# Gate and up projections: more steps as seven products of sums, with the split weights also in the residual's place

## The reference

```python
hn2 = rmsnorm(x, norm2_w[l])
gu = hn2 @ w_gate_up[l]                                     # 2048 x 2*5632
x = x + (jax.nn.silu(gu[..., :FFN_HIDDEN]) * gu[..., FFN_HIDDEN:]) @ w_down[l]
...
m = rms_norm(h, ffn_norm_g)
return h + (jax.nn.silu(m @ w_gate) * (m @ w_up)) @ w_down
```

## Time and profile before

| | us |
|---|---|
| median of 3 runs (2575.23 to 2576.02) | 2575.98 |
| the profiled execution's own time | 2576.22 |
| its span, first to last instruction | 2574.4 |

### The profile page before, as it was taken

The page is one execution under the profiler, slowest core; times in us unless marked ns, Lnnn a source line. Parts: engine busy times, 40 slices in busy tenths (PEclk is TensorE's granted clock), DMA queues, the critical chain, the costliest instruction groups (busy, mean ns, idle before and its releaser), DMA issues.

```text
span 2574.4 us, 30659 instructions
## 1 busy us (share of the span) xinstructions
PE 2561.0 (99%) x11740; PEld 2122.9 (82%) x11740; DVE 1603.7 (62%) x1799; ACT 1473.3 (57%) x1811; POOL 824.6 (32%) x368
## 2 busy tenths in 40 slices
PE   9999999999999999999999999999999999999999
PEld 7888888888887888888888888888878888888887
DVE  6798955434347878787533467456477878786222
ACT  7776645445455656566544575565565656566333
POOL 2687753344441000000444455333320000003443
PEclk9999999999999999999999999999999999999999
DMA  8766654466666475656566644554557565655554
GB/s 302 222 209 204 178 192 161 162 223 210 204 203 246 168 250 174 243 184 217 190 215 205 223 168 157 172 196 142 185 194 247 174 243 183 234 194 194 202 203 147
DMA packets 174705, 516.13 MB, mean 200 GB/s; under 512 B 108027, under 2 KB 111068, under 8 KB 117216
## 3 DMA queue, kind: packets, MB, share of 16 engines
q1 hardware_dynamic: 174128, 513.64, 59.9%
q10 hardware_dynamic: 432, 0.52, 0.1%
HBM read 487.38 MB, written 2.10 MB: 190 GB/s over the span
## 4 chain that ended last, share of the span: by engine, by line
PE 94%; DVE 2%; issue 1%; ACT 1%; POOL 1%; DMA 0%; SPq 0%; ACTq 0%; DVEq 0%; POOLq 0%
PE PB L858 18%; PE PB L862 18%; PE PB L859 18%; PE PB L925 8%; PE PB L926 8%; PE PB L929 8%; PE PB L909 2%; PE PB L906 2%; PE PB L904 2%; ACT WH L1460 1%; PE PB L1168 1%; PE PB L1010 0%; DVE WL L2251 0%; PE PB L1040 0%; POOL WL L3321 0%
## 5 line engine op out<-in xcount | busy, mean ns | idle before, releaser
L3321 POOL TENSOR_TENSOR WL<-RAW,WH 128x1024 fp32r<-128x1024 f32 x280 | 703.1, 2512 | 1730.0 <-ACT WH L1460 1729.1
L1460 ACT ACTIVATE WH<-RAW 128x1024 fp32r<-128x1024 f32 x738 | 776.2, 1057 | 797.6 <-PE PB L862 634.3
L2251 DVE TENSOR_TENSOR WL<-RAW,WH 128x1024 fp32r<-128x1024 f32 x456 | 613.6, 1348 | 753.6 <-ACT WH L1460 752.3
L858 PE MATMUL PB<-WH,HNH 128*128 128x512 f32 x1152 | 458.6, 398 | 2.6 <-ACT TM L2036 2.4
L862 PE MATMUL PB<-WL,HNH 128*128 128x512 f32 x1152 | 449.4, 390 | 1.5 <-POOL WL L3321 1.5
L859 PE MATMUL PB<-WH,HNL 128*128 128x512 f32 x1152 | 448.6, 389 | 0.0
L858 PE MATMUL PB<-WH,HDH 128*128 128x512 f32 x704 | 273.9, 389 | 0.0
L859 PE MATMUL PB<-WH,HDL 128*128 128x512 f32 x704 | 273.9, 389 | 0.0
L862 PE MATMUL PB<-WL,HDH 128*128 128x512 f32 x704 | 273.9, 389 | 0.0
L858 PEld LDWEIGHTS PB<-WH,HNH 128*128 128x128 f32 x1152 | 216.4, 188 | 50.5 <-ACT TM L2036 3.2
L862 PEld LDWEIGHTS PB<-WL,HNH 128*128 128x128 f32 x1152 | 216.2, 188 | 49.0 <-POOL WL L3321 3.4
(11 more groups left out here) (450 smaller groups left out, 3887.0 us busy)
## 6 DMA issues: line engine op xcount, KB each, us to landing
RAW<-in_w_gu SPq DMA_DIRECT2D x136, 1024.0 KB, 7.2
RAW<-in_w_dn SPq DMA_DIRECT2D x88, 1024.0 KB, 4.8
RAW<-in_w_in_a SPq DMA_DIRECT2D x53, 1024.0 KB, 5.2
RAW<-in_w_in SPq DMA_DIRECT2D x45, 1024.0 KB, 4.8
RAWX<-in_w_gu SPq DMA_DIRECT2D x40, 1024.0 KB, 6.6
RAW<-in_w_out SPq DMA_DIRECT2D x32, 1024.0 KB, 4.7
RAW<-in_w_ga SPq DMA_DIRECT2D x24, 1024.0 KB, 4.8
RAW<-in_w_gb SPq DMA_DIRECT2D x24, 1024.0 KB, 4.8
```

Of the source, the lines that this page charges most:

```text
L858: e.matmul(o, hi[:, k, x], WH[:, s, c], start=k == 0, stop=False)
L1460: e.activation(wh(key), source(key), ACT.Copy).then_inc(*wt.act.mark(("wh", *key)))
L2251: e.tensor_tensor(to, raw, hi, ALU.subtract).then_inc(*wt.dve.mark(("wl", *key)))
L3321: e.tensor_tensor(to, raw, hi, ALU.subtract).then_inc(*wt.pool.mark(("wl", *key)))
```

## The change

In even groups (j = 2, 4, 6, 8, 10) steps 0 and 2 are done as seven products, in odd groups step 1 as before (`steps_summed`). The seven come in another order: t1 before b22, with PSUM bank 5 before bank 3; the weight sums follow other remainders (`SUM_BEHIND`). The banks of the several-output products accumulate over both such steps, so in even groups they are taken out 32 tiles later (k = 82 and 96 to 108 for 50 and 64 to 76). The activation sums cover three of the four steps: 768 columns an operation for 256, 3072 for 1024, and in the first group they are rounded at tile 70 for 54 and their remainder taken at tile 75 for 60. They need the arena in which the three extra slots lay; one of the slots moves to 24 KB of the arena and two into the place of `X`. So `X` is stored to a tensor in HBM (`AWAY`) at tile 50 of group 0, and loaded again at tile 12 of the first down group.

```diff
-BLOCKS = ("b11", "b21", "b22", "t1", "t2", "t3", "t4")
-BANK_OF = (1, 2, 3, 5, 6, 7, 4)
-SUMMED = (1,)
-FIRST_PLAIN = 0
-SUM_BEHIND = {0: 3, 2: 4, 3: 5, 4: 6}
+BLOCKS = ("b11", "b21", "t1", "b22", "t2", "t3", "t4")
+BANK_OF = (1, 2, 5, 3, 6, 7, 4)
+SUM_BEHIND = {0: (2,), 3: (4, 5), 4: (6,)}
...
+def steps_summed(j):
+    return (1,) if j % 2 else (0, 2)
...
+        AWAY = nc.dram_tensor("away", (128, 2, 2048), F32).ap()
...
-        SAH = ar("SAH", [128, 4, 2, 128], 0, F32R)
-        SAL = ar("SAL", [128, 4, 2, 128], 4, F32R)
-        SAF = ar("SAF", [128, 4, 2, 128], 4)
-        HNS = ar("HNS", [128, 4, T], 8)
-        WHX = ar("WHX", [128, MORE, SU * 128], 8, F32R)
-        WLX = ar("WLX", [128, MORE, SU * 128], 20, F32R)
+        SAH = ar("SAH", [128, 4, 6, 128], 0, F32R)
+        SAL = ar("SAL", [128, 4, 6, 128], 12, F32R)
+        SAF = ar("SAF", [128, 4, 6, 128], 12)
+        HNS = ar("HNS", [128, 12, T], 64)
+        WX = [at(f"WX{i}", [128, 2, SU * 128], F32R, (arena + 24 * KB, xt_off, xt_off + 8 * KB)[i]) for i in range(MORE)]
...
+                        if j == 0 and k == 50:
+                            for h in range(2):
+                                e.wait_ge(*m.dve.done("x", before, 3, h))
+                            e.dma_start(AWAY[:, :, :], X[:, :, :]).then_inc(landed["x away"], 16)
...
+            def x_back(stage):
+                e.wait_ge(*wt.pe.done("nt", NT[{1: "gu1", 3: "gu2"}[stage]] + 43))
+                e.dma_start(X[:, :, :], AWAY[:, :, :]).then_inc(landed["x back"], 16)
...
+                last, begun = steps_summed(j)[-1], set()
+
+                def first(q):
+                    if q in begun:
+                        return False
+                    bank_free(q)
+                    begun.add(q)
+                    return True
...
                 for d in range(4):
-                    (seven if d in SUMMED else plain)(d)
+                    (seven if d in steps_summed(j) else plain)(d)
...
                 if key in first_in_slot:
                     e.wait_ge(*m.dve.done("sums", first_in_slot[key]))
+                    e.wait_ge(landed["x away"], 16 * (first_in_slot[key] + 1) // 2)
...
-                    if k == 54:
-                        sums_rounded()
...
-                run(64)
+                for k in tiles(64):
+                    if k == 6:
+                        sums_rounded()
...
-                        if k == 50:
-                            e.wait_ge(*wt.pe.done("unit", stage, j, SUMMED[-1], 0))
+                        if k == 32 * last + 18:
+                            e.wait_ge(*wt.pe.done("unit", stage, j, last, 0))
...
-                    if k == 60:
+                for k in tiles(64):
+                    if k == 11:
                         row_sums_low()
-                run(64)
...
+                    e.wait_ge(*x_back)
                     residual(dn, g)
```

More of the change, by code:

```diff
@@ L903, in seven @@
                             (hi, lo), c = left(i, d, r), slice(r * 512, (r + 1) * 512)
-                            e.matmul(banks[q][:, :], hi, wh(key)[:, c], start=r == 0 and q in (1, 5, 6, 7),
-                                     stop=False)
+                            e.matmul(banks[q][:, :], hi, wh(key)[:, c], start=start and r == 0, stop=False)
                             e.matmul(banks[q][:, :], lo, wh(key)[:, c], start=False, stop=False)
@@ L909, in seven @@
                             t = e.matmul(banks[q][:, :], hi, wl(key)[:, c], start=False,
-                                         stop=r == 1 and q in (1, 5, 6, 7))
+                                         stop=d == last and r == 1 and q in (1, 5, 6, 7))
                         t.then_inc(*wt.pe.mark(("unit", *key)))
@@ L918, in plain @@
                         u, q, x = (w.i - n % 8) // SU, ((2, 4), (3, 8))[up][h], slice(h * 128, (h + 1) * 128)
-                        if d == FIRST_PLAIN and pair == 0:
-                            bank_free(q)
+                        start = first(q)
                         if h == 0:
@@ L924, in plain @@
                             k, c = 4 * d + 2 * pair + r, slice(r * 512, (r + 1) * 512)
-                            e.matmul(banks[q][:, :], HNH[:, k, x], wh((u,))[:, c], start=k == 4 * FIRST_PLAIN, stop=False)
+                            e.matmul(banks[q][:, :], HNH[:, k, x], wh((u,))[:, c], start=start and r == 0, stop=False)
                             e.matmul(banks[q][:, :], HNL[:, k, x], wh((u,))[:, c], start=False, stop=False)
@@ L2009, in rounded @@
                     if j == 0:
-                        e.wait_ge(*wt.pe.done("unit", stage, 10, SUMMED[-1], 6))
-                    if j == 2:
+                        e.wait_ge(*wt.pe.done("unit", stage, 10, steps_summed(10)[-1], 6))
+                    if j == 6:
                         e.wait_ge(*wt.pe.done("product", stage, 10, 8))
@@ L2255, in weight_sum @@
                 s = stage, j, d
-                b11, b21, b22, b12 = (source((*s, b)) for b in range(4))
+                b11, b21, b12, b22 = (source((*s, b)) for b in range(4))
                 if BLOCKS[i] == "t1":
@@ L2277, in tiles @@
                         low(*key)
-                        if len(key) > 1 and key[3] in SUM_BEHIND:
-                            weight_sum(*key[:3], SUM_BEHIND[key[3]])
+                        for i in SUM_BEHIND.get(key[3], ()) if len(key) > 1 else ():
+                            weight_sum(*key[:3], i)
                     yield k
@@ L3069, in products_summed @@
                             *m.dve.mark(("u2", stage, j)))
-                    if k == 72:
-                        e.wait_ge(*wt.pe.done("unit", stage, j, SUMMED[-1], 5))
+                    if k == 40:
+                        e.wait_ge(*wt.pe.done("unit", stage, j, last, 5))
                         e.wait_ge(*m.dve.done("u2", stage, j))
@@ L3135, in ffn @@
                 for g in range(4):
+                    if g == 0:
+                        x_back = landed["x back"], 16 * (stage + 1) // 2
                     for k in tiles(4 * 44):
```

51 lines of the change are left out of this document (28 added, 23 removed).

## The result

| | us |
|---|---|
| changed kernel, median of 4 runs (2609.66 to 2613.37) | 2611.54 |
| kernel before, in the same session (2575.23 to 2576.97) | 2576.0 |
| ratio, with its 95% interval | 1.0138 [1.0125, 1.0151] |
| the profiled execution's own time, and its span | 2613.37, 2611.2 |

The kernel became 35.5 us **slower**, where 2571.8 was forecast with a range from 2561 to 2580. The profile's own span grew by 36.8 us (2574.4 to 2611.2).

A forecast was written before the change was run, and what follows sets the result against it. The number of matmuls on PE was taken to bound the kernel, unless another engine comes too late. 2576.2 - 13.6 (fewer matmuls) + 9.4 (stage starts) = 2572.0 us, as a median 2571.8, range 2561 to 2580.

The forecast's parts named there:

- the line on the ends: Boundaries even to odd, and group 10 to the down stage: cost 0, bound 1 us a stage.
- DVE's load: In the groups: DVE's 41.1 us against PE's 40.8 in an even group, but 74.2 in 83.0 over two groups.
- The start of a stage: Group 0 to group 1: PE stands 7.3 us against 2.6 now, 4.7 us more a stage, 9.4 for two.
- the walk: Operation-by-operation timing of DVE, POOL and ACT at a stage's start, ending at 801.7 with PE due at 794.4.
- the 60 matmuls: Five groups in each of two stages get one more step of seven: 60 x 0.2267 = 13.6 us less.
- the boundary odd to even: The next group's seven need bank 3, freed by the first `up_summed`: cost 0, bounds 0 and 0.9 us each of ten.
- the raw pair in an even group: Matrices for step 2 load after step 0's last remainder frees their buffers: cost 0, 2.4 us to spare.
- rival B: The raw pair's loop in even groups becomes the bound: 2.8 us late in each, 2599.8 us; chance 0.08.
- D: DMA bound by size, an even group no shorter than an odd one: 2585.4 us; chance 0.03 together with E, an unshortened-steps rival.
- A: The wait for `up_summed` at odd-to-even boundaries is real, 0.3 to 0.9 us ten times: 2574.8 to 2580.8; chance 0.16.
- S: Stage starts cost little, POOL's operations falling in DVE's gaps: 2562.4 us, or 2559.8 with -1.3 a stage; chance 0.23.
- The round trip of `X`: Store to HBM and load back, 2 MB each way, twice: cost 0; without the units split ahead 5 us a stage.

## Why the prediction was wrong

**The step that failed** is the line on the ends: "Even to odd a plain step wants bank 3 only 5.4 us in; group 10 to down, fewer units are due. Cost 0, bound 1 us a stage." It asked for one bank, that of `up_summed`. A plain step's first matmul goes to a gate bank, at once, and it is `gate_summed` that must have emptied it. The row for this was in the prediction's hands: in the earlier trace rows `gate_summed` starts at 836.27 and the group ends at 837.9, 1.6 us later, with the first of its two done about 1 us before. Two operations of 1.14 us more ahead of it are enough to spend that. I had walked odd to even, where the next group starts with seven, and let the other boundary go in one sentence. By the change's own table the plain start now stood behind the fullest group, and eight such boundaries at 2.34 us are 18.7 us.

**Group 10** was the same sentence's other half. Fewer units are due there, but hidden remainders (L3048) and POOL's first operation are too, and they stand ahead of `gate_summed`: 11.0 us in two for a bound of 1 a stage.

**The lower clock** had no term: 10.8 us at 0.427 for 0.227 us, all behind stops. It comes only with other stops, so it belongs to the price of each. It costs its full length only if PE need not wait again soon after: with the store early and the additions not, no slow matmul followed the stop near 777, and the next wait, for L3144, was 2.2 us for the 1.1 of the same kernel with the store at tile 50.

**DVE's load.** The busy time of the changed kernel in group 2 (columns as in the earlier trace rows, which had 33.12 us of 42.20):

```profile
840.60:881.40 40.80, 40.80 (x181) 33.38 (x179) 35.21 (x35) 27.61 (x29) 0.00 (x0) 1.00 0.69 241
```

DVE has 35.2 of 40.8, part of the 41.1 having moved into the odd groups as said; with `gate_summed` earlier the load is carried. What was wrong was to conclude from a mean over two groups that each single operation is in time.

**The start of a stage** was sized 4.7 us more for each; it measured 2.25 each. The mechanism was right: the remainder at 775.82 took 3.42, PE stood 2.0 us (777.07 to 779.29, less a regular step) where 2.2 were worked out, and the long remainder of the sums took 5.52. But L3144 ended at 799.5 where the walk had 801.7, so PE came 5.0 us late in all for 7.3. The whole difference was there before group 1: the sums' remainder ended at 786.3 where the walk had 788.8. The rows of POOL and ACT in the changed kernel show how:

```profile
774.97 3.18 POOL L3344 TENSOR_TENSOR WL<-RAW,WH 128x1024 fp32r<-128x1024 f32 x1 [5.13 <-ACT WH L1478]
775.93 2.77 ACT L2037 ACTIVATE SAH<-SAF 128x3072 fp32r<-128x3072 f32 x1 [1.04 <-DVE SAF L3068]
```

The walk put POOL's second operation ahead of the last two differences and let ACT round only from 778.2. It came later and fell on the weight remainder behind them, so that ACT could round while DVE was held. The silu's wait went, as said.

**Right, by these runs:** the 60 matmuls at 0.227 us; the boundary odd to even, 0 to 0.9 us each (measured 1.3 us in two of ten); the raw pair in an even group and DMA's size (no wait of PE in steps 2 and 3 of even groups, none for a load). So rival B, the slower one that was named, was not it, nor D; A's mechanism (`up_summed` too late) showed at its own boundary only as those 1.3 us. S had no cost at the starts; they cost 2.25 us each, which is the lower bound of the forecast. The round trip of `X` cost nothing that could be told in its own run, though the loads around its store landed later there too; only where DVE ran earlier did that make DVE wait, for 2.6 us in all.

**Left open:** whether two steps of seven in group 10 pay with `up_summed` ahead of the weight remainder that waits for ACT, and whether any order of DVE's and POOL's work at a stage's start would do without the last gaps; two were tried and came out alike.

## What to carry to other kernels

When a change gives tiles of unequal kind (here groups that start plain or with sums), walk every pair of neighbours, with the first buffer that the next one touches, and read from the trace how many microseconds its release has to spare today. An engine that is 86% busy can carry a load and still be late at one operation; ask what stands ahead of that operation in its order, and move it before taking work away. Price a new stop of PE at more than its length: here the 29.7 us of stops at the ends of groups (18.7 and 11.0) brought about another 9 at the lower clock.

## What was not expected of the hardware

PE's granted clock went from 1.00 to 0.50 after single stops of some microseconds, though PE was busy 98% of the span, and the page's clock row shows nothing of it (every slice is in the highest tenth). The length of the stop alone didn't decide: behind 2.2 us at 777.07 seven matmuls ran at the lower clock, behind 2.4 us at 881.19 none, behind 5.9 us at 1225.89 thirteen. The Trainium skill (TensorE: Matmul & The Clock Gate, "HAM oscillation — how this bites in real kernels") tells of a kernel in which waits for transfers bring TensorE back to the lower clock again and again; this trace shows the same behind waits for DVE. The same page, in "Wait — 56ns, not 53.3ns?", gives 426.7 ns from start to start at the lower level for 512 columns, with which the trace agrees (0.427 us), and 215.7 ns at the higher, where this trace has 226.7 (its matmuls each have a weight load of their own).

A POOL operation with nothing to do with DVE's data sets the length of a DVE operation: 1.2 us became 3.42 at 775.82 and again at 1221.80, and without POOL's the three additions took 3.50 for 5.69.
